# Closing and first projections moved into the experts' programs, and a reordered routing, in a two-block transformer kernel on one Trainium2 core

## What is computed

```python
h = layer_norm(DEEPNORM_ALPHA * h + m, ln1_g[l], ln1_b[l])
f = moe_ffn(h, w_router[l], b_router[l], w_exp_in[l], b_exp_in[l], w_exp_out[l], b_exp_out[l])
h = layer_norm(DEEPNORM_ALPHA * h + f, ln2_g[l], ln2_b[l])
...
logits = (t @ w_router + b_router).astype(jnp.float32)
top_val, top_idx = lax.top_k(logits, TOP_K)
gate_w = jax.nn.softmax(top_val, axis=-1).astype(h.dtype)
...
hb = xb @ w_exp_in[e] + b_exp_in[e]
g = jnp.minimum(hb[:, :D_FF], SWIGLU_LIMIT)
u = jnp.clip(hb[:, D_FF:], -SWIGLU_LIMIT, SWIGLU_LIMIT)
a = g * jax.nn.sigmoid(SWIGLU_ALPHA * g) * (u + 1.0)
return a @ w_exp_out[e] + b_exp_out[e]
...
h = x @ w_in[l]
(nsa_q, nsa_kc, nsa_vc, nsa_ks, nsa_vs, nsa_kw, nsa_vw, nsa_g, nsa_z, ...) = jnp.split(h, offsets, axis=-1)
```

## Time and profile before

| What | us |
|---|---|
| median of 3 runs | 2024.03 |
| lowest and highest | 2021.77, 2032.19 |
| the profiled execution | 2023.78 |
| its span, first to last instruction | 2022.0 |
| TensorE busy, share of the span | 1930.3 (95%) |
| routing, from its first transposes to the first expert product | 425.6 to 465.6 |
| experts, last block's products end | 1603.3 |
| closing, to the first projection | 1608.8 to 1625.1 |

### The profile page before, as it was taken

The page is one execution under the profiler, slowest core; times in us unless marked ns, Lnnn a source line. Parts: engine busy times, 40 slices in busy tenths (PEclk is TensorE's granted clock), DMA queues, the critical chain, the costliest instruction groups (busy, mean ns, idle before and its releaser), DMA issues. The chain is left out here.

```text
span 2022.0 us, 28752 instructions
## 1 busy us (share of the span) xinstructions
PE 1930.3 (95%) x10074; PEld 1546.7 (76%) x10074; DVE 1576.5 (78%) x1787; ACT 1230.7 (61%) x1319; POOL 291.1 (14%) x172
## 2 busy tenths in 40 slices
PE   6989899979999999999999999999999798999898
PEld 5667688757888888888888888888888685687776
DVE  6662541479999999999999999999999865654787
ACT  3444432336777777777777777777777535653551
POOL 0103044110121111122112121211111100000100
PEclk9999999998999999999999999999999998999899
DMA  6322333459999999999999999999999742001222
GB/s 212 91 84 63 79 94 104 146 204 356 361 387 382 394 375 391 377 391 392 381 392 375 391 379 388 387 380 397 372 394 376 251 114 68 22 32 63 64 65 83
DMA packets 201804, 518.44 MB, mean 256 GB/s; under 512 B 22134, under 2 KB 81694, under 8 KB 201388
## 3 DMA queue, kind: packets, MB, share of 16 engines
q1 hardware_dynamic: 191548, 482.70, 64.2%
q0 software_dynamic: 9360, 34.08, 6.6%
q10 hardware_dynamic: 832, 0.80, 0.1%
HBM read 494.43 MB, written 28.88 MB: 259 GB/s over the span
## 5 line engine op out<-in xcount | busy, mean ns | idle before, releaser
L2005 PE MATMUL bank<-moe_upper,x_hi 128*128 128x512 f32 x1504 | 603.3, 401 | 0.2 <-DVE x_hi L2220 0.2
L2007 PE MATMUL bank<-moe_upper,x_hi 128*128 128x512 f32 x1504 | 585.9, 390 | 0.0
L2226 DVE TENSOR_TENSOR beyond_lower<-beyond,moe_upper 128x2048 fp32r<-128x2048 f32 x192 | 434.9, 2286 | 31.9 <-ACT moe_upper L2128 31.9
L2128 ACT CAST moe_upper<-beyond 128x2048 fp32r<-128x2048 f32 x192 | 367.5, 1915 | 140.9 <-PE bank L2007 136.3
L2005 PEld LDWEIGHTS bank<-moe_upper,x_hi 128*128 128x128 f32 x1504 | 282.5, 188 | 62.7 <-issue 0.7
L2007 PEld LDWEIGHTS bank<-moe_upper,x_hi 128*128 128x128 f32 x1504 | 282.3, 188 | 59.8
L2006 PE MATMUL bank<-beyond_lower,x_hi 128*128 128x512 f32 x752 | 293.0, 390 | 0.0
L2226 DVE TENSOR_TENSOR mixed_t_lower<-mixed_t,moe_upper 128x2048 fp32r<-128x2048 f32 x96 | 218.3, 2286 | 27.0 <-ACT moe_upper L2128 26.9
L2128 ACT CAST moe_upper<-above 128x2048 fp32r<-128x2048 f32 x96 | 183.7, 1914 | 72.9 <-PE bank L2007 72.9
L2226 DVE TENSOR_TENSOR above_lower<-above,moe_upper 128x2048 fp32r<-128x2048 f32 x96 | 218.2, 2285 | 6.3 <-ACT moe_upper L2128 6.3
L2128 ACT CAST moe_upper<-mixed_t 128x2048 fp32r<-128x2048 f32 x96 | 183.9, 1916 | 58.1 <-PE bank L2007 56.2
(11 more groups left out here) (632 smaller groups left out, 3409.3 us busy)
## 6 DMA issues: line engine op xcount, KB each, us to landing
beyond<-in_w_exp_in_dram SPq DMA_DIRECT2D x128, 1024.0 KB, 8.1
mixed_t<-in_w_exp_in_dram SPq DMA_DIRECT2D x64, 1024.0 KB, 8.2
above<-in_w_exp_in_dram SPq DMA_DIRECT2D x64, 1024.0 KB, 8.0
beyond<-in_w_exp_out_dram SPq DMA_DIRECT2D x64, 1024.0 KB, 9.1
mixed_t<-in_w_exp_out_dram SPq DMA_DIRECT2D x32, 1024.0 KB, 7.4
above<-in_w_exp_out_dram SPq DMA_DIRECT2D x32, 1024.0 KB, 9.4
ahead<-in_w_in_dram SPq DMA_DIRECT2D x23, 512.0 KB, 5.3
ahead<-in_w_in_dram SPq DMA_DIRECT2D x3, 1536.0 KB, 6.6
```

The source lines that it names most:

```text
L2005: nc.tensor.matmul(to, hi[:, f, :], upper[u][:, t, cols], start=f == 0 and not biased, stop=False)
L2007: done = nc.tensor.matmul(to, lo[:, f, :], upper[u][:, t, cols], start=False, stop=f == NK - 1)
L2128: nc.scalar.copy(upper[h % SPLIT][:, :, :], ring[s][:, :, :]).then_inc(hi_ready, 1)
L2226: nc.vector.tensor_tensor(lower[s][:, :, :], ring[s][:, :, :], upper[h % SPLIT][:, :, :].bitcast(F32), ALU.subtract).then_inc(lo_ready, 1)
```

## The change

*Routing.* SyncE loads the three copies of the bias rows first, saves the first three tiles, loads two pieces, saves the fourth tile, and loads five more; the eighth piece waits for the first gathered rows. The gain and shift of the next norm are loaded after the second block's pieces. GpSimd makes the biases' remainder right after the router weights', ahead of its wait for the weights; the transposes of the masks then wait for both of its results (`share_ready` 2). TensorE gets one dummy product of 512 columns ahead of the fourth tile's transposes, one of 256 behind them, and five instead of six behind the placement products. VectorE makes the comparison `before` behind the token numbers. The semaphore `logits_t` is replaced by a second count of `logits_ps`.

*Closing.* `closing_stage` becomes `closing_programs`: it hands out its four programs, and the experts' `last` calls them at the end of each engine's own, so the block between is gone. GpSimd makes three of the four remainders of `close_lower`, and TensorE waits for them at column groups 2, 4 and 6. The additions of the halves also give row sums (`tensor_tensor_reduce`), the right half's starting from the left's; ScalarE makes sums of squares of (left sum less 512 times the value), from which the variance follows by a formula in place of the statistics. Rows are normalised left halves first, and TensorE's transposes of the first four column groups wait for those alone. ScalarE loads the table for the root earlier, by a root of a constant.

```diff
         for i in range(READY):
             save(i)
-        for g in range(3):
-            sp.dma_start(full[NE * g:NE * g + NE, :], A["b_exp_out"][0]).then_inc(bias_in, 16)
-        for h in range(4):
+        for h in range(2):
             load(h)
         save(READY)
-        for h in range(4, INNER):
+        load(2)
+        for h in range(3, INNER - 1):
             load(h)
         sp.wait_ge(r.rows_sem[0], 16)
+        load(INNER - 1)
...
         turn(READY, 0)
         turn(READY, 1)
+        keep_busy(nc, k, 7, (256,))
...
             def last(rest):
-                pool.wait_ge(w_hi, hi0 + 4)
-                close_lower(nc.gpsimd, 3)
+                for h in (1, 2, 3):
+                    pool.wait_ge(w_hi, hi0 + h + 1)
+                    close_lower(nc.gpsimd, h).then_inc(r.closing.late_split, 1)
+                    pool.drain()
...
-            pe.wait_ge(normed, (m + 1) * NT)
+            pe.wait_ge(left_normed, left0 + NT)
             for c in range(4):
                 turn(c)
+            pe.wait_ge(normed, (m + 1) * NT)
             for f in range(NK):
+                if f in (2, 4, 6):
+                    pe.wait_ge(late_split, f // 2)
...
+            def squares_of(h, i, ready):
+                act.wait_ge(r.sums_ready, ready)
+                nc.scalar.activation(r.ring[4 + h][:, i // 2, halves[i % 2]], x[:, i, halves[h]], ACT.Square, scale=-512.0,
+                                     bias=left_sum[:, i:i + 1], accum_out=squares[:, h, i:i + 1]).then_inc(squared, 1)
...
-            for i in (1, 3):
-                nc.scalar.activation(x[:, i, :], x[:, i, :], ACT.Identity, scale=norm.r[:, i:i + 1],
-                                     bias=offset[:, i:i + 1]).then_inc(normed, 1)
+            for half, done in zip(halves, (left_normed, normed)):
+                for i in (1, 3):
+                    nc.scalar.activation(x[:, i, half], x[:, i, half], ACT.Identity, scale=norm.r[:, i:i + 1],
+                                         bias=offset[:, i:i + 1]).then_inc(done, 1)
...
+            def add_rows(h, i, start, total):
+                dve.wait_ge(r.summed, NT * h + i + 1)
+                nc.vector.tensor_tensor_reduce(x[:, i, halves[h]], r.mixed(i)[:, halves[h]], k.bank[SUM_BANKS[h][i]][:, :],
+                                               1.0, start, ALU.add, ALU.add, total[:, i:i + 1]).then_inc(r.sums_ready, 1)
...
             for i in range(NT):
-                nc.vector.tensor_tensor(x[:, i, 512:D], r.mixed(i)[:, 512:D], k.bank[SUM_BANKS[1][i]][:, :], ALU.add)
-                statistics(nc, k, i, (0,))
-                dve.drain()
-                statistics(nc, k, i, (1,))
+                dve.wait_ge(r.mixed_in[i], 16)
+                add_rows(0, i, 0.0, left_sum)
+                if i == 0:
+                    right_rest()
             dve.drain()
-            norm.variance(dve, 0, NT).then_inc(var_ready, 1)
+            for i in range(NT):
+                add_rows(1, i, left_sum[:, i:i + 1], row_sum)
```

More of the change, by code:

```diff
@@ L2467, in _ @@
[L2467 to L2469 removed]
+            nc.vector.tensor_tensor(offset[:, :], minus_mean[:, :], norm.r[:, :], ALU.mult).then_inc(scaled, 1)
+            for half, done in zip(halves, (left_normed, normed)):
+                for i in (0, 2):
+                    nc.vector.tensor_scalar(x[:, i, half], x[:, i, half], minus_mean[:, i:i + 1], norm.r[:, i:i + 1],
+                                            ALU.add, ALU.mult).then_inc(done, 1)
```

120 lines of the change are left out of this document (72 added, 48 removed).

## The result

| Kernel, runs | median us | lowest to highest | ratio to before | 95% interval |
|---|---|---|---|---|
| before, 7 | 2022.51 | 2021.77 to 2032.19 | | |
| changed, 7 | 2014.62 | 2010.60 to 2018.71 | 0.995 | 0.9936 to 0.9963 |
| changed, second comparison, 6 | 2012.84 | 2009.51 to 2013.97 | 0.9943 | 0.9930 to 0.9957 |

The forecast was 2013.6 us and a gain of 10.4. By the first ratio the gain is 10.1 us, with an interval from 7.5 to 12.9; by the second, beside 11 runs of before with a median of 2023.83, 11.5 (8.7 to 14.2). The gain is the ratio's, not the difference of the medians: those differ by 7.9 us in the first comparison and by 11.0 in the second. The first ratio lies on the bound of 0.5% itself.

A forecast was written before the change was run, and what follows sets the result against it. TensorE, busy 95% of 2022.0 us, bounds the kernel; the gain lies in its waits in routing and closing part. 4.0 + 6.4 = 10.4 us off 2023.8, plus 0.2 between profile and median, gives 2013.6 us; range 2010.5 to 2019.0.

The forecast's parts named there:

- Bias remainder: Routing: GpSimd's remainder of the output biases, moved earlier, no longer holds up VectorE's small cast; 2.16 us gained, bounds 0.9 and 2.2.
- Comparison: Routing: moving `before` (0.95 us) behind the token numbers takes it out of VectorE's chain; 0.8 us gained.
- Router clock: Routing: new dummy products fill TensorE's two idle gaps and hold its clock up through the router; 1.2 us, bounds 0 and 1.4.
- five dummies suffice: Routing: `hot` comes 7.3 us behind the placement products, and six dummies had ended 7.0 us behind them.
- Rival 3: Dummies don't hold the clock: router and closing transposes run at the low level, 1.2 + 1.2 us less, 2016; chance 0.20.
- Clock at the start of the expert products: End of routing: expert products, arriving earlier, may run a little at the lower clock; 0.2 us subtracted, bounds 0 and 0.8.
- The gather: Routing: GpSimd's gather began 1.2 us after the token numbers; meeting the moved comparison was costed at nothing, at most 0.95 us.
- The other moves here cost nothing: Routing: reordered bias loads, saves, weight piece 7 and gain and shift loads cost nothing on the path.
- rival 2: First expert's loads: deferred weight piece 7 lands late and stalls TensorE, slower than before, for example 2034 us; chance 0.05.
- Routing, 4.0: Sum for the routing: 2.16 + 0.8 + 1.2 - 0.2 = 4.0 us gained.
- Closing, 6.4: Closing part: transposes start at 1615.2 against 1621.61, 6.4 us gained and carried to the first projection; bounds 5.0 and 7.2.
- Rival 1: Closing part: GpSimd's three remainders shut out VectorE's eight sums at the shared port, up to 6.4 us lost, say 2018; chance 0.13.

The follow-up runs named there:

- close_only: The kernel before with only the closing part of the change, its routing left as it was: 2018.47 us, ratio 0.9973 (0.9961 to 0.9984).

## Why the prediction was right, and where it wasn't

*What bounds.* Right: the loop is not touched, 1134.8 to 1136.3 us in all, and the whole gain stands at the two places.

*Bias remainder, 2.16 us.* Measured 2.16 at the cast, and 2.17 at the list products when it is undone. The Trainium skill's rule of the shared port (SBUF — State Buffer, the two sides) and the trace agree again: both plain remainders that stood beside GpSimd's took 2.76 and 2.77 us, and GpSimd's 3.91 and 3.35 where VectorE was there first, against 2.40 for those that met none.

*Comparison, 0.8.* Measured 0.82.

*Router clock, 1.2.* Measured 1.21, and 1.23 when undone. The argument that five dummies suffice took their time from before; with the later fall they came within 0.1 us of delaying the list products. Rival 3's first half falls, eleven profiles to three. Its second half was right as to the state and wrong as to the price: the closing's clock did fall (dummies 3.38 us), but a held clock gives back only 0.4 us, not 1.2, since ScalarE's halves are next.

*Clock at the start of the expert products, 0.2.* Too small. From the rows' landing to the tenth product before takes 5.9 us and the changed routing 6.3 in the mean: 0.4 more on average, 0.8 in the first profile.

*The gather, unpriced.* The token numbers come 4.16 us earlier, the rows only 3.7 in the mean, since the gather then takes 4.4 to 5.7 us from its start instead of 4.5. It meets more weight traffic because it comes earlier. The sum lacked this term of 0.4. It took over the gather's time of before, in which the queues were empty. That this came out nearly right is luck: it held only because piece 7 was deferred, which the forecast priced at nothing.

*"The other moves here cost nothing."* This step failed by what it left out. Piece 7 was looked at only as a danger (rival 2), and the price of not deferring it was never worked out. Undone, it costs 1.2 to 2.7 us of the 3.4 that the routing gains. The danger itself was none: the piece landed 9.9 us after its issue, and ScalarE's wait ahead of it is for TensorE as before.

*Routing, 4.0.* Measured 3.4 in the mean of the six profiles with this routing (2.7 to 3.9).

*Closing, 6.4.* Measured 6.6 in the mean, 6.9 in the first profile. The steps in between were met within 0.5 us behind the first row product: last sum 6.84 (forecast 6.8), variance at 8.44 (8.8), left halves at 11.6 (11.8), transposes 11.7 (12.1), first projection 15.1 (15.6). ScalarE ended the wait, as said. Rival 1 falls, as shown above. The parts, each undone by itself in the changed kernel, so that they need not add: 4.3 the statistics, 1.1 the remainders, 0.3 the halves. About 0.9 remains for the rest. That it is the block boundary above all is not shown; the boundary was not tried alone.

*The sum.* 10.4 forecast; 3.4 + 6.6 = 10.0 by stretches, and 10.1 and 11.5 by the two comparisons. An error of 0.6 in the routing and one of 0.2 the other way in the closing part. That the point came within 1.0 us of the median is partly luck: the base was one profile and three runs of a program whose executions differ by 9 us, and before's median moved from 2024.03 in three runs to 2022.51 in seven.

## What to carry to other kernels

When a step is pulled ahead of background transfers, price the transfer that it meets there, and look at what the queue may hold back for it: here an order of loads that seemed neutral kept between a third and four fifths of the routing's gain. Where one engine makes sums while its statistics follow, put the squares on an idle neighbour; here the chain shortened by 4.3 us where the statistics had taken about 5.5. Compare two profiles by stretches counted from a common instruction, since one execution against another hid half of the gain.

## What the runs showed of the hardware that I had not expected

The clock of TensorE falls for short times in places that differ between executions of one program, also ahead of the change: at the span's 62.8, 134.5 and 380 us in one, at 129 alone in the other. The start of the routing, the same code in all fourteen, lay between 423.80 and 428.71 us. A difference of 0.005 in the mean granted clock over 2010 us is 20 us at the lower level instead of the upper, in which a full stream loses 10; the two spans differ by 9.2.

The 16 list products of 96 columns take 3.10 us at the upper level and took 3.12 in before, mostly at the lower one: for these narrow products the level made no difference. In all fourteen profiles the clock fell 26.3 to 27.4 us behind the routing's start, though the list products begin 22.8 us behind it in ten of them, at 24.0 and 25.0 in two and at 26.2 in two. In before and close_only TensorE had idled 2.5 us just ahead of those products; in the ten the list products were over, behind a gap of at most 0.65 us. One dummy of 512 columns between the two groups did not prevent the fall. What sets its place stays open.
